# Scan kernel: the pieces of Gram, turns and y issued in four parts between the products of the inverse

## What is computed

```
def _wkv7_step(S, inp):
    r_t, w_t, k_t, v_t, aa_t, bb_t = inp
    sa = jnp.einsum('zbhij,zbhj->zbhi', S, aa_t)
    S = S * w_t[..., None, :] + sa[..., :, None] * bb_t[..., None, :] + v_t[..., :, None] * k_t[..., None, :]
    y = jnp.einsum('zbhij,zbhj->zbhi', S, r_t)
    return S, y
...
    S0 = jnp.zeros((2, b, N_HEADS, HEAD_DIM, HEAD_DIM), f32)
    _, ys = lax.scan(_wkv7_step, S0, seq)
```

## Time and profile before

| what | value |
|---|---|
| median of 3 runs | 4458.7 us (4452.56 to 4463.43) |
| the profiled execution | 4469.37 us, its span 4467.6 us, mean granted clock 0.964 |
| PE, PEld, DVE, ACT, POOL busy over the span | 91%, 78%, 48%, 31%, 30% |
| the scan | from about 2275 to 3265 us, 990 us |
| in it PE, PEld, DVE, ACT, POOL busy | 816, 750, 726, 544, 577 us |

### The profile page before, as it was taken

How to read it: one execution, slowest core, us unless ns; L and a number is a source line. 1 busy time by engine, 2 the same in 40 slices (tenths; PEclk the granted TensorE clock), 3 DMA queues, 4 the chain that set the end, 5 groups by cost and what they waited for, 6 DMA issues and landing times. The chain is left out here.

```text
span 4467.6 us, 108489 instructions
## 1 busy us (share of the span) xinstructions
PE 4079.3 (91%) x47874; PEld 3470.3 (78%) x47874; DVE 2157.8 (48%) x3506; ACT 1387.1 (31%) x2945; POOL 1344.8 (30%) x933
## 2 busy tenths in 40 slices
PE   5999798999999997899948888888868999999999
PEld 5889567888888886788747777777757888888888
DVE  4662462353352442546747777777743253242351
ACT  3331472211111112234435555555532211011111
POOL 3111233211111113422145566566523311111111
PEclk8999899999999998999979999999979999999999
DMA  4222433212213113122232222222143212313213
GB/s 124 70 79 73 119 93 110 69 38 85 85 38 116 55 44 107 60 79 71 94 100 78 67 80 80 67 81 75 51 147 106 91 38 65 104 36 97 74 37 108
DMA packets 399059, 356.42 MB, mean 80 GB/s; under 512 B 62912, under 2 KB 370112, under 8 KB 396544
## 3 DMA queue, kind: packets, MB, share of 16 engines
q1 hardware_dynamic: 389888, 345.60, 25.0%
q10 hardware_dynamic: 8704, 3.88, 0.4%
HBM read 247.16 MB, written 102.24 MB: 78 GB/s over the span
## 5 line engine op out<-in xcount | busy, mean ns | idle before, releaser
L423 POOL TENSOR_TENSOR f_wlow<-f_raw,f_whigh 128x1024 fp32r<-128x1024 f32 (+1 forms) x152 | 359.9, 2368 | 1677.2 <-ACT f_whigh L512 1677.2
L492 PE MATMUL f_ps<-fx_hh,f_whigh 128*128 128x512 f32 (+1 forms) x2112 | 530.4, 359 | 0.0
L492 PE MATMUL f_ps<-fx_hl,f_whigh 128*128 128x512 f32 (+1 forms) x2112 | 529.3, 359 | 0.0
L492 PE MATMUL f_ps<-fx_hh,f_wlow 128*128 128x512 f32 (+1 forms) x2112 | 528.7, 358 | 0.0
L512 ACT ACTIVATE f_whigh<-f_raw 128x1024 fp32r<-128x1024 f32 (+1 forms) x152 | 156.6, 1030 | 891.9 <-PE f_ps L492 864.4
L492 PEld LDWEIGHTS f_ps<-fx_hl,f_whigh 128*128 128x128 f32 x2112 | 349.4, 189 | 65.5
L492 PEld LDWEIGHTS f_ps<-fx_hh,f_whigh 128*128 128x128 f32 x2112 | 349.4, 189 | 65.0
L492 PEld LDWEIGHTS f_ps<-fx_hh,f_wlow 128*128 128x128 f32 x2112 | 349.0, 189 | 65.3
L579 DVE TENSOR_TENSOR f_xo<-f_ps,f_xo 128x512 f32<-128x512 f32 x168 | 90.7, 596 | 625.7 <-PE f_ps L492 593.6
L492 PE MATMUL f_ps<-mo_oh,f_whigh 128*128 128x512 f32 (+1 forms) x1440 | 362.6, 360 | 25.4 <-POOL f_wlow L423 25.4
L492 PE MATMUL f_ps<-mo_ol,f_whigh 128*128 128x512 f32 (+1 forms) x1440 | 360.0, 358 | 0.0
(11 more groups left out here) (291 smaller groups left out, 8496.0 us busy)
## 6 DMA issues: line engine op xcount, KB each, us to landing
f_xo<-xres SPq DMA_DIRECT2D x64, 640.0 KB, 3.9
xres<-f_xo SPq DMA_DIRECT2D x48, 640.0 KB, 2.9
f_raw<-in_ffn_w_gate SPq DMA_DIRECT2D x44, 512.0 KB
f_raw<-in_ffn_w_up SPq DMA_DIRECT2D x44, 512.0 KB
sc_rk<-rkvl SPq DMA_DIRECT2D x80, 256.0 KB
rkvl<-ri_ot SPq DMA_DIRECT2D x28, 640.0 KB
f_raw<-in_ffn_w_down SPq DMA_DIRECT2D x32, 448.0 KB
qkv_raw<-in_na_w_qkv SPq DMA_DIRECT2D x24, 512.0 KB, 5.5
```

What stands on the lines that cost most here:

```text
L423: nc.gpsimd.tensor_tensor(wlow[:, m % 2, 0:kt], raw[:, 0:kt], whigh[:, m % 2, 0:kt].bitcast(F32), ALU.subtract).then_inc(cut_lo, 1)
L492: last = nc.tensor.matmul(ps[:, m % 2, n, 0:count], w[:, m % 2, k], x[:, k, t0:t0 + count], start=(k == 0 and w is whigh and x is xh), sto ...
```

## The change

`gram`, `turn` and `y_products` are cut in four parts q each. For Gram a part is one of two products for one chunk (2 products); for turns the records of a chunk (4) or its values (2); for y the state's share of a chunk (4) or the two other shares (8). Their waits are taken out into functions of their own and stand ahead of the slot's inverse. `inverse` gets the part as `side_work` and calls it behind each chunk's products. Gram's first piece, which stood behind slot 0's inverse, is mixed into it like the others. `lora` and `bonus` stay ahead of the inverse. No other engine's list changes. (Some of a semaphore's names in the order below are those of an earlier stage that used the same one: `ri_end_floored` and `ri_end_inverted` are `a_pt[0]` and `a_pt[1]`, `ri_end_spread` is `a_turn[0]`, `ri_key_stored` is `a_x`.)

```
@@ gram, turn @@
-                def gram(G, z, half):
-                    r = G % 4
+                def gram_waits(G, z, half):
                     if half == 0 and z == 0:
                         pe.wait_ge(d_rec, G + 1)
                         pe.wait_ge(g_r, G + 1)
...
                     elif half == 0:
                         pe.wait_ge(d_gram[0], G + 1)
-                    for s in (2 * half, 2 * half + 1):
-                        u = unit(z, s)
-                        for a in range(2):
-                            for rows in halves:
...
-                    if half:
+
+                def gram(G, z, half, q):
+                    r, s, a = G % 4, 2 * half + q // 2, q % 2
+                    u = unit(z, s)
+                    for rows in halves:
...
+                    if half and q == 3:
                         last.then_inc(pe_gram[z], 1)
...
+                def turn(G, z, half, q):
+                    r, s = G % 4, 2 * half + q // 2
+                    u = unit(z, s)
+                    if q % 2 == 0:
                         for a in range(2):
                             for rows in halves:
                                 nc.tensor.matmul(turn_ps[z][rows, 0, a * W + s * C:a * W + (s + 1) * C], rec[rows, r, z, u, a], ident[rows, rows],
                                                  start=True, stop=True)
...
+                        return
+                    for rows in halves:
+                        last = nc.tensor.matmul(turn_ps[z][rows, 1, s * C:(s + 1) * C], vb[rows, r, z, u * C:(u + 1) * C], ident[rows, rows],
+                                                start=True, stop=True)
+                    if half and q == 3:
                         last.then_inc(pe_turn[z], 1)
@@ inverse @@
-                def inverse(G, n):
+                def inverse(G, n, side_work=None):
                     if not group(G) or n > 2 * INV:
+                        if side_work is not None:
+                            for s in range(U):
+                                side_work(s)
                         return
...
                         for h in range(2):
                             if does_t:
                                 last_t = level_t(G, 1 - zp, kt, s, h)
+                        if side_work is not None:
+                            side_work(s)
                     if does_p:
                         last_p.then_inc(pe_p[zp], 1)
@@ y_products @@
+                def y_products(G, half, q):
+                    s = 2 * half + q // 2
...
+                    if q % 2 == 0:
+                        for h, rows, z, out in places:
+                            nc.tensor.matmul(out, st[rows, g, z], rec[rows, G % 4, z, unit(z, s), 3], start=True, stop=False)
+                        return
+                    for h, rows, z, out in places:
+                        nc.tensor.matmul(out, tu[rows, g, z], nr[rows, G % 4, z, 0, s], start=False, stop=False)
+                    for h, rows, z, out in places:
+                        last = nc.tensor.matmul(out, vt[rows, G % 2, z, s], nr[rows, G % 4, z, 1, s], start=False, stop=True)
+                    if half and q == 3:
                         last.then_inc(pe_y, 1)
@@ the slots @@
-                        if n == 1 and group(I + 2):
-                            gram(I + 2, 0, 1)
+                        side_work = None
+                        if n in (0, 1, 3, 6) and group(I + 2):
+                            z, half = {0: (0, 0), 1: (0, 1), 3: (1, 0), 6: (1, 1)}[n]
+                            gram_waits(I + 2, z, half)
+                            side_work = lambda q: gram(I + 2, z, half, q)
...
                         if n in (4, 5) and group(I - 1):
-                            y_products(I - 1, n - 4)
-                        if n in (7, 8) and group(I + 1):
-                            turn(I + 1, 0, n - 7)
-                        if n in (9, 10) and group(I + 1):
-                            turn(I + 1, 1, n - 9)
+                            if n == 4:
+                                y_waits(I - 1)
+                            side_work = lambda q: y_products(I - 1, n - 4, q)
+                        if n in (7, 8, 9, 10) and group(I + 1):
+                            z, half = divmod(n - 7, 2)
+                            turn_waits(I + 1, z, half)
+                            side_work = lambda q: turn(I + 1, z, half, q)
                         if n == 11 and group(I + 3):
                             bonus(I + 3)
-                        inverse(I + 1, n)
-                        if n == 0 and group(I + 2):
-                            gram(I + 2, 0, 0)
+                        inverse(I + 1, n, side_work)
```

More of the change, by code:

```diff
@@ L1649, in gram, with turn_waits @@
                         pe.wait_ge(d_gram[0], G + 1)
[L1650 to L1656 removed]
+                def gram(G, z, half, q):
+                    r, s, a = G % 4, 2 * half + q // 2, q % 2
+                    u = unit(z, s)
+                    for rows in halves:
+                        last = nc.tensor.matmul(gram_ps[rows, a, s * 128:(s + 1) * 128], rec[rows, r, z, u, a],
+                                                rec[rows, r, z, u, 2:4].rearrange("p a n -> p (a n)"), start=True, stop=True)
+                    if half and q == 3:
                         last.then_inc(pe_gram[z], 1)
[L1659 to L1660 removed]
+                def turn_waits(G, z, half):
                     if half == 0 and z == 0:
[L1662 removed]
+                        pe.wait_ge(v_in[G % 4], 32 * (G // 4 + 1))
                         if group(G + 2):
@@ L1769, in s_product @@
                     last.then_inc(pe_s, 1)
[L1771 to L1777, removed]
-                            pe.wait_ge(a_turn[0], min(G + 2, NG))
-                    for s in (2 * half, 2 * half + 1):
-                        g = (4 * G + s) % (2 * U)
-                        to = [slice(unit(z, s) * C, (unit(z, s) + 1) * C) for z in range(Z)]
-                        for h, rows in enumerate(halves):
-                            for z in range(Z):
-                                nc.tensor.matmul(y_ps[side(h, z), z, to[z]], st[rows, g, z], rec[rows, G % 4, z, unit(z, s), 3], start=True, stop=False)
-                        for h, rows in enumerate(halves):
-                            for z in range(Z):
-                                nc.tensor.matmul(y_ps[side(h, z), z, to[z]], tu[rows, g, z], nr[rows, G % 4, z, 0, s], start=False, stop=False)
-                        for h, rows in enumerate(halves):
-                            for z in range(Z):
-                                last = nc.tensor.matmul(y_ps[side(h, z), z, to[z]], vt[rows, G % 2, z, s], nr[rows, G % 4, z, 1, s], start=False, stop=True)
-                    if half:
@@ new lines, in y_waits @@
+                def y_waits(G):
+                    pe.wait_ge(a_u, 4 * G + 4)
+                    if group(G + 4):
+                        pe.wait_ge(a_tanh, G + 5)
+                    else:
+                        pe.wait_ge(d_bonus, NG)
+                        pe.wait_ge(a_turn[0], min(G + 2, NG))
+                def y_products(G, half, q):
+                    s = 2 * half + q // 2
+                    g = (4 * G + s) % (2 * U)
+                    to = [slice(unit(z, s) * C, (unit(z, s) + 1) * C) for z in range(Z)]
+                    places = [(h, rows, z, y_ps[side(h, z), z, to[z]]) for h, rows in enumerate(halves) for z in range(Z)]
+                    if q % 2 == 0:
[7 more added lines that the diff above has]
+                    if half and q == 3:
```

14 lines of the change are left out of this document (4 added, 10 removed).

## The result

The changed kernel takes 4519.3 us, the median of 4 runs (4517.5 to 4522.0); the kernel before, beside it on the same chip, 4455.6 us (4449.0 to 4463.4). The ratio is 1.0143, with a 95% interval of 1.0124 to 1.0162. The profiled execution took 4521.98 us.

The account below looks back on a forecast made before the run. Instruction supply was taken to bound slots 4 to 10, the chain of results slots 0 to 3. 1.1 + 0.5 = 1.6 us in each of 38 iterations adds 61 us to 4458.7, giving 4520 us; 8-in-10 range 4472 to 4585.

Parts of the forecast that it names:

- Two kinds of slot: Scan iteration: instruction supply sets the pace in slots 4 to 10, the chain of results in slots 0 to 3.
- what a block costs at least: PE's instruction fetch: a block of about 254 rows takes at least 4.26 or 3.85 us, the spacing of stall ends.
- Mixing itself, put at zero: All mixed slots: alternating inverse and side-piece products on the array costs nothing by itself.
- Slots 0 and 1, 0.75 us: Inverse waits for the record and then lacks the side piece's cover; next chain product at 2811.25, before 2810.51.
- my 0.8: Between inverse steps: 0.8 us from issue of the last first-step product through drain and ACT's copy to the next inverse.
- Slots 2 and 3, 0.75 us: Gram's second piece ends with slot 1, delaying DVE's masks and add, so slot 3's inverse; slots 0 to 3 cost 1.5 us.
- Slot 3's inverse starts 1 us later after x: Sign in the next profile that the forecast is right: slot 3's inverse starts 1 us later after x than before.
- 1.1 taken: Slots 0 to 3: of 1.5 us some is absorbed by the block reaching into slot 4; bounds 1.0 and 1.5.
- Slots 4 to 10, waits of 2.45 us, of which 0.5 stays: Lost cover adds waits, 1.0 us in slot 7; fetch stalls absorb most, bounds 0 and 2.45 us.
- Supply hides nearly everything: Blocks of slots 0 to 3 also have slack, leaving 0.0 to 0.6 us: 4459 to 4482 us, chance 0.18.
- Nothing is hidden: Issue stalls keep their length, waits add whole, 2.9 to 3.95 us an iteration: 4569 to 4609 us, chance 0.14.
- It gets faster: Slots 4 and 5: spread order brings blocks and fetches into step, 0 to -55 us: 4404 to 4459, chance 0.06.

Follow-up runs that it names:

- wide turns: Kernel before, and also changed kernel, with two 64-column turn products replaced by one of 128 columns, second record left out: 0.9933, and 1.0082 in the changed kernel.
- half y: Kernel before with y's 48 products cut from 64 to 32 columns, half of y left out, same rows (also before_half_y): 4475.8 us, ratio 1.0010.
- after_0_behind: Changed kernel with Gram's first piece back behind slot 0's inverse, the other nine pieces mixed: 4531.8 us, ratio 1.0144 to the kernel before.
- gated: Kernel before with the inverse's waits ahead of whole side pieces, nothing mixed, slot 0's Gram still behind the inverse: 4521.3 us, ratio 1.0112.
- after_1_6_ahead: Changed kernel with Gram's pieces of slots 1 and 6 whole and ahead of the inverse again: 4514.9 us, ratio 1.0092 to the kernel before.
- y_mixed: Kernel before with only the two y pieces (slots 4 and 5) mixed into the inverse: 4467.1 us, ratio 1.0000.
- after_7_ahead: Changed kernel with slot 7's turns piece whole and ahead of the inverse, the other nine pieces mixed: 4529.1 us, ratio 1.0144 to the kernel before.

## Why the prediction was right, and where its steps were not

**What bounds the kernel.** Two kinds of slot, supply in 4 to 10 and the chain of results in 0 to 3: right, by the wide turns and the half y. That 3.85 to 4.26 us is "what a block costs at least" was too simple. Spacings that end in a stall have a mean of 3.93 us in before, but 4.22 in the changed kernel and 4.34 in after_0_behind (from the starts of PE's rows). Why a block costs more there stays open.

**Mixing itself, put at zero.** Most of the loss is there without it (gated). Some 0.3% is left for it, with the bounds of nothing and 0.65%, of which slot 7's part is a matter of order and not of the array: Gram mixed into slot 6 ends the slot, and DVE's strict mask waits for it.

**Slots 0 and 1, 0.75 us.** Measured 0.67. Slot 0's inverse starts 0.52 us after the x products, where I had said about 0.6. For slot 1 the size was right and half of the reason wrong: the step "POOL's factors for this step aren't later than before" is true, but they bound slot 1 already. In the changed kernel the copy's way does (the last group of first-step rows in slot 0 starts at 2972.76 and its last row 0.06 us later, slot 1's inverse at 2973.52, so 0.7 us for my 0.8):

```profile
2972.76 0.28 PE L1699 MATMUL sc_inv_ps<-sc_tf,sc_bl 64*64 64x64 f32 x4
2972.87 0.28 PE L1654 MATMUL sc_gram_ps<-sc_rec 64*64 64x128 f32 x2
...
2973.52 0.27 PE L1699 MATMUL sc_inv_ps<-sc_tf,sc_bl 64*64 64x64 f32 x2
...
2973.09 0.38 ACT L1905 ACTIVATE sc_pt<-sc_inv_ps 128x256 f32<-128x256 f32 x1 [1.19 <-PE sc_inv_ps L1699]
```

**Slots 2 and 3, 0.75 us.** Measured 0.56, and by another way. The strict mask does wait for the whole of slot 1, as predicted (it starts at 2975.14, after Gram's last rows at 2974.70). But the inclusive mask and the add follow it in 2.31 us, not in the 2.48 that I had carried over, and slot 3's inverse starts 0.81 us after its x products, as good as before (0.77), released by the copy:

```profile
2977.07 0.30 PE L1751 MATMUL sc_chain_ps<-sc_vt,sc_ga 64*64 64x64 f32 x8
...
2977.88 0.27 PE L1699 MATMUL sc_inv_ps<-sc_tf,sc_bl 64*64 64x64 f32 x2 [0.40 <-ACT sc_pt L1905]
...
2977.40 0.38 ACT L1905 ACTIVATE sc_pt<-sc_inv_ps 128x256 f32<-128x256 f32 x1
...
2975.14 0.42 DVE L2047 TENSOR_TENSOR sc_bm<-sc_gram_ps,sc_m_strict 128x256 f32<-128x256 f32 x1 [1.79 <-PE sc_gram_ps L1654]
...
2977.45 0.28 DVE L2092 TENSOR_TENSOR sc_tf<-sc_inv_ps,sc_tf 128x128 f32<-128x128 f32 x1
```

DVE's add ends at 2977.73, only 0.05 us ahead of the copy. That the copy alone would hold the inverse there is seen in after_1_6_ahead: with the strict mask early again, slot 3's inverse still starts 0.81 us after its x products.

The cost is the Gram piece itself. Before, most of its 0.88 us ran inside these 0.77; now it comes after them. "Slot 3's inverse starts 1 us later after x" was wrong; the inverse is later only by what slots 0 and 1 had lost. It didn't follow from my own working either, by which x too is 0.75 us later and the inverse comes 1.0 us after it for 0.76. Slots 0 to 3 together: 1.24 us for 1.5 by the working and 1.1 taken. That 1.1 lies near is in part luck: the working was 0.26 too high, and the 0.4 that I took off as absorbed is not seen in these slots.

**Slots 4 to 10, waits of 2.45 us, of which 0.5 stays.** The largest, 1.0 us in slot 7 behind DVE's strict mask, is there as described:

```profile
2986.26 0.32 PE L1654 MATMUL sc_gram_ps<-sc_rec 64*64 64x128 f32 x2
2986.32 0.38 PE L1765 MATMUL sc_chain_ps<-sc_xs,sc_rf 64*64 64x64 f32 x6
2987.39 0.27 PE L1699 MATMUL sc_inv_ps<-sc_tf,sc_bl 64*64 64x64 f32 x2 [0.69 <-DVE sc_tf L2092]
...
2986.62 0.42 DVE L2047 TENSOR_TENSOR sc_bm<-sc_gram_ps,sc_m_strict 128x256 f32<-128x256 f32 x1 [1.67 <-PE sc_gram_ps L1654]
2986.97 0.28 DVE L2092 TENSOR_TENSOR sc_tf<-sc_inv_ps,sc_tf 128x128 f32<-128x128 f32 x1
```

Gram's last rows, then the mask, the add, the inverse 1.18 us behind the u products at 2986.21. The other slots gave most of it back, by 1.47 us less stall in an iteration. In the two profiles slots 4 to 10 grew by 0.23 us and slot 11 shrank by 0.18, so the absorption looks larger than the 2 us that I had taken. Against the 25 iterations of before at full clock slots 4 to 10 grew by 0.52 us (15.31 to 15.83), the 0.5 that I had taken, and slot 11 shrank by 0.16.

**The sum.** 1.6 us by 38 iterations was to give 61, and the medians differ by 63.7. The two profiles show only 1.28 us, 49 by 38 iterations, and their spans differ by 52.6. The profiled execution of before, 4469.4 us, lies 14 above the median beside the changed kernel; the prediction had set the 11 us to its own median aside. The prediction also had no term for the clock. Against the 25 iterations of before at full clock the changed kernel's are 1.60 us longer (25.47 for 23.87), against all 33 only 1.28. These 25 leave out the longest stalls, so 1.60 is the upper of the two bounds. By the medians an iteration lost 1.6 to 1.7 us, of which the firm slots 0 to 3 are 1.24. The rest of about 0.4 agrees with the 0.5 taken, but rests on that difference and on the iterations at full clock. The prediction's total is right, then, with slots 2 and 3 sized 0.2 us too high in their working, one reason (slot 3) wrong, and a clock of which it said nothing.

**The other cases.** "Supply hides nearly everything" failed in slots 0 to 3, which hold no stall to hide in. "Nothing is hidden" failed by the 48 us that issue idle lost. "It gets faster" rested on a y piece that empties a block in slots 4 and 5; y_mixed tests the y pieces by themselves and gives 1.000. The fall of issue idle, foretold as 20 to 60 us, was 48.5; the iteration 25.5 us for 25.8.

## What to carry to other kernels

A piece of independent work ahead of a dependent step is not only "in the way": ask which wait it covers, also where no idle time is shown because the piece itself fills it. Spread between the step's products, it comes behind the wait, and its time is paid. Where small products keep the queue fed at its limit, an order that saves or loses a few tenths of a microsecond in such a stretch is mostly evened out by the stalls, in both directions; fewer instructions are what shortens it.

## What the runs showed of the hardware that I had not expected

Undoing one slot's loss brought nothing back that can be measured: after_0_behind and after_7_ahead removed 0.28 and 0.47 us from their slots (0.24% and 0.40% of the time) and both have 1.0144, for 1.0143 of the changed kernel on another chip. For the first of them the intervals of 0.2% don't decide it. The stalls rose from 2.54 to 3.28 and 3.06 us in an iteration. I had expected a block to have a fixed least price, at which half would stay won; the runs don't tell what sets that price. The instruction count is the sturdier lever, in either order: 64 of 1497 rows fewer took off 0.67% before the change and about 0.6% (1.0143 to 1.0082, on two chips) after it.

TensorE's clock fell in the middle of the scan, where PE is in flight for 82% of the time. In 8 of 33 iterations of before the granted clock was 0.50 for 3.4 us, from about the end of an "issue" stall of 2.05 us or more. In before_half_y, with less work in the array, it fell in 15 of 33; the longest stalls of these 15 iterations are 1.42 to 3.29 us, and five iterations with one of 2.21 to 2.47 kept the clock, so the length of the stall alone doesn't tell. The changed kernel, whose stalls stay at 1.65 us or less, never lost it. The mean over the whole program shows little of this: it went from 0.964 to 0.968.
